# Seven early norms: the factor as a power on GpSimd in place of a root on ScalarE and a reciprocal on VectorE

## The chip, the cores and the metric

The kernel runs on one core of one Trainium2 chip. The metric is the device time of one execution in microseconds (us), the median of several runs. Less is better. The engines are TensorE (PE in the rows; PEld is its weight load), VectorE (DVE), ScalarE (ACT), GpSimd (POOL) and SyncE (SP), which issues most of the loads.

## The reference, cut to what matters

The reference is two transformer-like blocks on 512 tokens with a model width of 1024, all in float32. Every sublayer begins with a root-mean-square norm over the width:

```python
def rms_norm(x, g):
    xf = x.astype(jnp.float32)
    y = xf * lax.rsqrt(jnp.mean(xf * xf, axis=-1, keepdims=True) + EPS)
    return (y * g.astype(jnp.float32)).astype(x.dtype)
```

The norms that the change touches stand before the two feed-forward parts of the first block, before its short convolution, at its end (`norm_one`), and in the second block before the cross attention, before the feed-forward part and at the end. What follows a norm is, but for `norm_one` and the last one, a product of all 1024 normalised columns with a weight matrix, so no product can begin before the norm has its factor.

## The kernel before, in words

Activations are kept transposed: the 128 partitions hold columns of the model, the free dimension holds the 512 tokens, and the 1024 columns are KD = 8 tiles of 128 x 512. `X` is the residual stream. `XN` is the normalised tile, and it lies in the buffer `HXF`, as do the squares of a norm before it. `XNH` and `XNL` are its high and low parts: the products are made of three float32r products, high by high, low by high and high by low (`split_product`, L688 to L690, and for the first two units after a norm `split_pair`, L703 to L705). The weights are split on VectorE into `WH` (L714) and `WL` (L716), one unit of 128 x 1024 at a time, two units ahead of TensorE. SyncE loads the weights into a ring of slots.

Each engine has its own program, and the order of work on each engine is the order in which it is written there; engines meet only at semaphores. A `NormStage` holds the semaphores and the steps of one norm. In a norm with `early=True` the work goes so:

- ScalarE writes the square of each tile of `X` as it is finished (L596, `norm_act_squares`), eight squares.
- GpSimd adds squares 1 to 6 onto square 0 (L625, `norm_pool`), six additions, each after the one before and after its square.
- TensorE multiplies the sum and square 7 by a matrix of ones (L634, `norm_pe`), so that each partition of bank 6 holds the sum over the whole width for the 512 tokens.
- ScalarE takes the root of that sum over 1024 plus EPS into `ROOT` (L600, `norm_act_root`).
- VectorE takes the reciprocal of `ROOT` into `RSTD` (L640, `norm_dve`) and then multiplies the eight tiles of `X` by `RSTD` (L649, where a gain and a shift are applied by ScalarE at L608, and L651, where the gain is applied in the same instruction). The low parts (L647) are put between these multiplications; ScalarE makes the high parts (L617).

`RSTD` and `ROOT` are one buffer each of 768 columns, and all norms share them. Eleven norms go through `norm_act_root` and `norm_dve`. The seven with `early=True` are `norm_ffn[0]`, `norm_sc`, `norm_ffn[1]`, `norm_one`, `norm_x2`, `norm_ffn2` and `norm_last`; the four others (`norm_lat`, `norm_ctx`, `norm_mix2`, `norm_mem2`) have no part on GpSimd. Of the latter, `norm_mix2` follows `norm_one` directly, and `norm_mem2` follows `norm_x2` on VectorE and ScalarE.

GpSimd's program has little else in these stretches. The four norms of the first block stand one after another in one loop, after them come the masks of the recurrent layer (L941) and four loads by DMA, and then the three norms of the second block. A sequence of additions in that program waits for ScalarE's squares, as it does before.

The lines from 1205 to 1265 and from 1515 to 1615 are TensorE's program around the norms, in the order `feed_forward(0)`, `norm_sc`, the short convolution, `feed_forward(1)`, `norm_one`, `norm_mix2`, then the recurrent and the attention layer, and then `norm_x2`, the cross attention, `norm_ffn2`, the feed-forward part, `norm_last` and the transposes of the output (L1617).

Of the kernel before, what the change touches and what calls it, by code (L numbers as in the profile page):

```python
# [8 lines left out]
ALU = mybir.AluOpType  # L9
ACT = mybir.ActivationFunctionType  # L10
# [4 lines left out]
P = 128  # L15
D = 1024
KD = D // P
T = 512
# [93 lines left out]
class Progress:  # L112
# [4 lines left out]
    def __init__(self, sem, steps, loop=False):  # L117
        self.sem, self.steps, self.n = sem, steps.split(), len(steps.split())
        self.credit, self.at = self.n if loop else 0, 0
# [88 lines left out]
class NormStage:  # L208
# [3 lines left out]
    def __init__(self, prog, name, shifted, parts=False, early=False):  # L212
        ks = range(KD)
        act = [[f"mod{k}"] if shifted else [] for k in ks]
        dve = [[f"n{k}"] for k in ks]
        for k in ks if parts else ():
            act[min(k + 1, KD - 1)].append(f"hi{k}")
            dve[min(k + 3, KD - 1)].append(f"l{k}")
        self.act_steps, self.dve_steps = sum(act, []), sum(dve, [])
        self.act = prog(f"{name}_act", " ".join([f"sq{k}" for k in ks] + ["root"] + self.act_steps))  # L220
        self.pe = prog(f"{name}_pe", "ssq")
        self.dve = prog(f"{name}_dve", " ".join(["rstd"] + self.dve_steps))
        self.pool = prog(f"{name}_pool", " ".join(f"a{k}" for k in range(1, KD - 1))) if early else None
        self.shifted = shifted

        self.out = self.act if shifted else self.dve
        self.written = self.out.done(f"mod{KD - 1}" if shifted else f"n{KD - 1}")
# [21 lines left out]
def two_blocks(nc, a, consts_d, bias_d, out):  # L249

    ctx = ExitStack()
    with ctx:
        def sb(name, n, parts=P):
            return ctx.enter_context(nc.sbuf_tensor(name, [parts, n], F32))

        def sem(name):
            return ctx.enter_context(nc.semaphore(name))

        def prog(name, steps, loop=False):
            return Progress(sem(name), steps, loop)  # L260
# [25 lines left out]
        bank = [PS[:, b, :] for b in range(8)]  # L286

        def banks(b, n):

            return PS[:, b:b + n, :].rearrange("p b n -> p (b n)")  # L290
# [11 lines left out]
        HX = HXF[:, :].rearrange("p (k t) -> p k t", k=KD)  # L302
        XN = cut(HXF, 0, KD, T)
        W = sb("W", SLOTS * SLOT)[:, :].rearrange("p (s n) -> p s n", s=SLOTS)
        EPSC = sb("EPSC", 3)
        ROOT, RSTD = sb("ROOT", TA), sb("RSTD", TA)
        SILU_C = sb("SILU_C", 2 * KD)[:, :].rearrange("p (k w) -> p k w", w=2)
        MOD = sb("MOD", 2 * N_MOD)
# [271 lines left out]
        def start_credit(eng, which):  # L580
            for p in LOOPS[which]:
                eng.sem_inc(p.sem, p.credit)


        def norm_act(act, st, src, sq, tokens, b, dst=None, gain=None, shift=None, ready=None):


            norm_act_squares(act, st, src, sq, ready)
            norm_act_root(act, st, tokens, b)
            norm_act_out(act, st, dst, gain, shift)  # L590
# [6 lines left out]

        def norm_act_root(act, st, tokens, b):
            act.wait_ge(st.pe.sem, st.pe.done("ssq"))
            nc.scalar.activation(ROOT[:, 0:tokens], bank[b][:, 0:tokens], ACT.Sqrt,  # L600
                                             bias=EPSC[:, 0:1], scale=1.0 / D).then_inc(st.act.sem, st.act.step("root"))

        def norm_act_out(act, st, dst=None, gain=None, shift=None):
# [15 lines left out]
        def norm_pool(pool, st, sq):  # L619

            for k in range(1, KD - 1):
                pool.wait_ge(st.act.sem, st.act.done(f"sq{k}"))
                if k > 1:
                    pool.wait_ge(st.pool.sem, st.pool.done(f"a{k - 1}"))
                nc.gpsimd.tensor_tensor(sq[:, 0, :], sq[:, 0, :], sq[:, k, :], ALU.add).then_inc(st.pool.sem, st.pool.step(f"a{k}"))  # L625

        def norm_pe(pe, st, sq, tokens, b):

            for k in (0, KD - 1) if st.pool else range(KD):
                if st.pool and k == 0:  # L630
                    pe.wait_ge(st.pool.sem, st.pool.done(f"a{KD - 2}"))
                else:
                    pe.wait_ge(st.act.sem, st.act.done(f"sq{k}"))
                mm = nc.tensor.matmul(bank[b][:, 0:tokens], ONES, sq[:, k, :], start=(k == 0), stop=(k == KD - 1))  # L634
            mm.then_inc(st.pe.sem, st.pe.step("ssq"))

        def norm_dve(dve, st, src, dst, tokens, gain=None):

            dve.wait_ge(st.act.sem, st.act.done("root"))
            nc.vector.reciprocal(RSTD[:, 0:tokens], ROOT[:, 0:tokens]).then_inc(st.dve.sem, st.dve.step("rstd"))  # L640
            dve.wait_ge(st.dve.sem, st.dve.done("rstd"))
            for step in st.dve_steps:
                k = int(step[1:])
                if step.startswith("l"):
                    dve.wait_ge(st.act.sem, st.act.done(f"hi{k}"))
                    normed, hi, lo = st.split
                    ins = nc.vector.tensor_tensor(lo[:, k, :], normed[:, k, :], hi[:, k, :], ALU.subtract)  # L647
                elif st.shifted:
                    ins = nc.vector.tensor_tensor(dst[:, k, :], src[:, k, :], RSTD[:, 0:tokens], ALU.mult)  # L649
                else:  # L650
                    ins = nc.vector.scalar_tensor_tensor(dst[:, k, :], src[:, k, :], gain[:, k:k + 1], RSTD[:, 0:tokens],  # L651
                                                         ALU.mult, ALU.mult)
                ins.then_inc(st.dve.sem, st.dve.step(step))
# [220 lines left out]
        def _(pool):  # L874
# [53 lines left out]
                        DT["dta"][:, d, 0:NT, ds(i * 2 + e, 1)].broadcast_to([P, NT, P]), ALU.mult).then_inc(sl_pool.sem, sl_pool.step(f"d{q}"))  # L928
            for st in (norm_ffn[0], norm_sc, norm_ffn[1], norm_one):
                norm_pool(pool, st, XN)  # L930


            def level_masks(i, at, p_pe, p_dve, p_pool):
# [21 lines left out]
                    nc.gpsimd.dma_start(DBIAS[:, e, :, :], by_pair[i, e]).then_inc(dbias_in, 16)  # L955
            for st in (norm_x2, norm_ffn2, norm_last):
                norm_pool(pool, st, XN)

        @block.tensor
        def _(pe):  # L960
# [26 lines left out]


            norm_pe(pe, norm_lat, XN_SQ, T, 6)
            norm_pe(pe, norm_ctx, CX_SQ, TC, 5)  # L990

            pe.wait_ge(in_act.sem, in_act.done("cols"))
# [629 lines left out]
        def _(act):  # L1622
# [21 lines left out]
            norm_act_squares(act, norm_lat, X, XN_SQ)  # L1644
            norm_act_squares(act, norm_ctx, CX, CX_SQ)
            norm_act_root(act, norm_lat, T, 6)
            act.wait_ge(norm_lat.dve.sem, norm_lat.dve.done("rstd"))
            norm_act_root(act, norm_ctx, TC, 5)
            act.wait_ge(ada_dve.sem, ada_dve.done("gainc"))
            norm_act_out(act, norm_lat, HX[:, :, 0:T], GAIN[:, 0, :], MOD[:, 0:KD])  # L1650
# [5 lines left out]
            for j in range(NPAIR):  # L1656
# [5 lines left out]

                nc.scalar.activation(ROOT[:, 0:T], bank[6], ACT.Sqrt, bias=EPSC[:, 1:2]).then_inc(hy_act.sem, hy_act.step(f"root{j}"))
            act.wait_ge(freed[ring.slot("hy_in", 8)], ring.used("hy_in", 8))
            nc.scalar.activation(KRAW, banks(4, 2)[:, 0:TA], ACT.Copy).then_inc(hy_act.sem, hy_act.step("k"))
            nc.scalar.activation(KSQ, banks(4, 2)[:, 0:TA], ACT.Square).then_inc(hy_act.sem, hy_act.step("ksq"))
            act.wait_ge(hy_pe.sem, hy_pe.done("kssq"))
            nc.scalar.activation(ROOT[:, 0:TA], banks(6, 2)[:, 0:TA], ACT.Sqrt, bias=EPSC[:, 0:1], scale=1.0 / HEAD).then_inc(hy_act.sem, hy_act.step("kroot"))

# [59 lines left out]
            for g in range(2):  # L1729
                act.wait_ge(gn_pe.sem, gn_pe.done(f"ssq{g}"))  # L1730
                nc.scalar.activation(DIFF[:, g, :], bank[g], ACT.Sqrt, bias=EPSC[:, 0:1], scale=1.0 / (2 * P)).then_inc(gn_act.sem, gn_act.step(f"root{g}"))

# [72 lines left out]
            def pair_pass(i, at, p_pe, p_act, p_dve, ahead):  # L1805
# [36 lines left out]
                act.wait_ge(p_pe.sem, p_pe.done("var", at))  # L1842
                nc.scalar.activation(ROOT[:, 0:T], bank[1], ACT.Sqrt, bias=EPSC[:, 2:3], scale=1.0 / HEAD).then_inc(p_act.sem, p_act.step("groot"))

# [95 lines left out]
        def _(dve):  # L1940
            start_credit(dve, "dve")
            nc.vector.memset(EPSC[:, 0:1], EPS)
            nc.vector.memset(EPSC[:, 1:2], HEAD * EPS).then_inc(in_dve.sem, in_dve.step("eps"))
            def ada_step(name, u, i, k, sums, before):

                s = ring.slot(name, u)
                dve.wait_ge(landed[s], ring.arrived(name, u, i))
                if u >= before:
                    dve.wait_ge(freed[ring.slot(name, u - before)], ring.used(name, u - before, i))
                else:  # L1950
                    dve.wait_ge(freed[ring.slot(name, u - before)], ring.free(name, u - before + SLOTS, i))
                nc.vector.scalar_tensor_tensor(sums, W[:, s, 0:D], SILU_C[:, ds(k, 1), 0], sums, ALU.mult, ALU.add).then_inc(freed[s], 1)
# [4 lines left out]
            for block, name in enumerate(("ada_shift", "ada_scale")):  # L1957
                with dve.Fori(0, 2) as i:
                    for u in range(4):
                        s, k, at = ring.slot(name, u), i * 4 + u, i + 2 * block  # L1960
# [54 lines left out]
            for j in range(XBC_TILES):  # L2015
                dve.wait_ge(freed[ring.slot("hy_in", 9 + j)], ring.used("hy_in", 9 + j))
                b = 2 * (j % 3)
# [242 lines left out]
            with dve.Fori(0, 2) as i:  # L2260
                for f in range(4):
                    b, o = 3 * (f % 2), CV[:, f % 2, :]
# [52 lines left out]
            r, k, v = (PRKV[:, u, :] for u in range(3))  # L2315
# [164 lines left out]
            with dve.Fori(0, KD) as i:  # L2480
                for u in range(4):
# [3 lines left out]
                    name, gate = (("r", SGR), ("a", SGA))[u - 2]  # L2485
# [86 lines left out]
```

## Time and profile before

| | |
|---|---|
| Time, median of three runs | 3348.53 us (3348.12 to 3349.93) |
| The profiled execution's own time | 3347.87 us |
| Its span, first to last instruction | 3346.2 us |
| Mean granted TensorE clock | 0.911 of full speed |
| PE, DVE, ACT and POOL busy | 89%, 49%, 20% and 6% of the span |
| Reciprocals of the norms (L640) | 11, nine of them over 512 tokens |
| Additions of squares on GpSimd (L625) | 42, mean 1.285 us |

The profile's page shows busy time and the chain of work that ended last. The chain is followed back from the last instruction to whatever released each step, so a piece that stands in it was not covered by anything else. In the timeline a row gives the start, the length, the engine, the line and the operation, and in brackets how long the engine had been idle and what ended that. The execution's own time is 1.67 us above its span.

### The profile page before, as it was taken

The numbers are of one execution on the slowest core, as the hardware profiler recorded it, in microseconds if no ns is written. First come the engines' busy times: TensorE is split into PE (matmuls) and PEld (weight loads), VectorE is DVE, ScalarE is ACT, GpSimd is POOL, SyncE is SP. The second block draws the span as 40 slices with busy tenths as digits, with TensorE's granted clock in tenths as the row PEclk, the third lists the DMA queues.
The fourth block names the chain that finished last, engine by engine and source line by source line (L and its number), as shares of the span: only waits on it lengthen the run. The fifth ranks groups of instructions, "written<-read, shape, count | busy, mean of one in ns | idle before, by whom it ended". The sixth has DMA issues, their size and how long they took to land.

```text
span 3346.2 us, 44820 instructions
## 1 busy us (share of the span) xinstructions
PE 2977.0 (89%) x17401; PEld 2135.4 (64%) x17401; DVE 1642.6 (49%) x2188; ACT 671.3 (20%) x1114; POOL 189.8 (6%) x227
## 2 busy tenths in 40 slices
PE   5998886799998989999879898888969988889998
PEld 3453464388886878888445555545537766768886
DVE  7555556344445554444356555622045453355554
ACT  3212321121101021110223333312131121121111
POOL 3010011000000000000001100100000000000000
PEclk8987666899999999999989999987969989999999
DMA  7443400233332323333110011020203322223332
GB/s 241 144 143 115 131 24 0 63 88 90 95 95 84 94 76 94 94 95 93 41 29 22 23 36 29 22 70 25 67 12 82 91 69 70 69 81 95 94 94 69
DMA packets 406147, 255.20 MB, mean 76 GB/s; under 512 B 23863, under 2 KB 391056, under 8 KB 405904
## 3 DMA queue, kind: packets, MB, share of 16 engines
q1 hardware_dynamic: 397824, 226.85, 23.4%
q0 software_dynamic: 6928, 21.89, 2.0%
q10 hardware_dynamic: 1280, 4.78, 0.4%
q8 instruction: 90, 1.47, 0.2%
q14 instruction: 25, 0.20, 0.0%
HBM read 250.60 MB, written 2.10 MB: 76 GB/s over the span
## 4 chain that ended last, share of the span: by engine, by line
PE 83%; DVE 9%; issue 4%; ACT 2%; DMA 1%; DVEq 0%; POOL 0%; ACTq 0%; POOLq 0%; SPq 0%
PE PS L688 12%; PE PS L690 12%; PE PS L689 12%; PE PS L675 9%; PE PS L1297 5%; PE PS L703 3%; PE PS L705 3%; PE PS L704 3%; PE PS L1083 2%; PE PS L1474 1%; PE PS L1466 1%; PE PS L1372 1%; PE PS L1064 1%; PE PS L1340 1%; PE PS L1074 1%
## 5 line engine op out<-in xcount | busy, mean ns | idle before, releaser
L714 DVE CAST WH<-W 128x1024 fp32r<-128x1024 f32 x304 | 210.9, 694 | 724.0 <-PE PS L690 551.1
L716 DVE TENSOR_TENSOR WL<-W,WH 128x1024 fp32r<-128x1024 f32 x304 | 372.7, 1226 | 10.4
L689 PE MATMUL PS<-XNL,WH 128*128 128x512 f32 x864 | 340.6, 394 | 0.0
L675 PE MATMUL PS<-HXF,W 128*128 128x512 f32 (+2 forms) x640 | 260.2, 567 | 19.9 <-ACT HXF L608 7.1
L690 PE MATMUL PS<-XNH,WL 128*128 128x512 f32 x704 | 277.5, 394 | 0.0
L688 PE MATMUL PS<-XNH,WH 128*128 128x512 f32 x704 | 277.3, 394 | 0.0
L689 PE MATMUL PS<-HL,WH 128*128 128x512 f32 x672 | 261.5, 389 | 0.0
L688 PE MATMUL PS<-HH,WH 128*128 128x512 f32 x672 | 261.5, 389 | 0.0
L690 PE MATMUL PS<-HH,WL 128*128 128x512 f32 x672 | 261.4, 389 | 0.0
L675 PEld LDWEIGHTS PS<-HXF,W 128*128 128x128 f32 (+1 forms) x640 | 122.6, 193 | 157.3 <-issue 152.1
L703 PE MATMUL PS<-XNH,WH 128*128 128x512 f32 x448 | 180.6, 403 | 32.8 <-DVE XNL L647 32.8
L704 PE MATMUL PS<-XNL,WH 128*128 128x512 f32 x480 | 193.5, 403 | 0.0
L689 PEld LDWEIGHTS PS<-XNL,WH 128*128 128x128 f32 x864 | 162.5, 188 | 38.3
L1297 PE MATMUL PS<-HXF,W 128*128 128x512 f32 x336 | 172.7, 653 | 11.5 <-DVE ARENA L2358 11.5
L705 PE MATMUL PS<-XNH,WL 128*128 128x512 f32 x448 | 179.1, 400 | 0.0
L625 POOL TENSOR_TENSOR HXF<-HXF 128x512 f32<-128x512 f32 x42 | 54.0, 1285 | 1965.3 <-ACT HXF L596 1965.3
L690 PEld LDWEIGHTS PS<-XNH,WL 128*128 128x128 f32 x704 | 132.2, 188 | 31.2
L688 PEld LDWEIGHTS PS<-XNH,WH 128*128 128x128 f32 x704 | 132.2, 188 | 31.0
L688 PEld LDWEIGHTS PS<-HH,WH 128*128 128x128 f32 x672 | 126.1, 188 | 26.3
L689 PEld LDWEIGHTS PS<-HL,WH 128*128 128x128 f32 x672 | 126.1, 188 | 26.3
L690 PEld LDWEIGHTS PS<-HH,WL 128*128 128x128 f32 x672 | 126.1, 188 | 26.2
L596 ACT ACTIVATE HXF<-X 128x512 f32<-128x512 f32 x72 | 44.7, 630 | 459.2 <-DVE X L2243 227.3
(454 smaller groups left out, 4818.5 us busy)
## 6 DMA issues: line engine op xcount, KB each, us to landing
W<-in_ada_w SPq DMA_DIRECT2D x64, 512.0 KB, 4.2
W<-in_ffn_w SPq DMA_DIRECT2D x64, 512.0 KB, 4.1
W<-in_w_in SPq DMA_DIRECT2D x58, 512.0 KB, 3.9
W<-in_ffn_w_gate SPq DMA_DIRECT2D x44, 512.0 KB, 3.8
W<-in_ffn_w_up SPq DMA_DIRECT2D x44, 512.0 KB, 3.8
ARENA<-in_ada_w POOLq DMA_DIRECT2D x32, 512.0 KB, 5.0
W<-in_ffn_w_down SPq DMA_DIRECT2D x32, 512.0 KB, 4.0
W<-in_sc_w_in SPq DMA_DIRECT2D x24, 512.0 KB, 3.7
```

Of the source, the lines that this page charges most:

```text
L625: nc.gpsimd.tensor_tensor(sq[:, 0, :], sq[:, 0, :], sq[:, k, :], ALU.add).then_inc(st.pool.sem, st.pool.step(f"a{k}"))
L675: mm = nc.tensor.matmul(dst, w[:, k, :], rhs(k), start=(start and k == 0), stop=(stop and k == kts - 1))
L688: nc.tensor.matmul(dst, WH[:, h, c], hi(k), start=(start and k == 0), stop=False)
L689: nc.tensor.matmul(dst, WH[:, h, c], lo(k), start=False, stop=False)
L690: mm = nc.tensor.matmul(dst, WL[:, h, c], hi(k), start=False, stop=(stop and k == kts - 1))
L703: nc.tensor.matmul(dst[u], WH[:, h, c], hi(k), start=(k == 0), stop=False)
L704: nc.tensor.matmul(dst[u], WH[:, h, c], lo(k), start=False, stop=False)
L705: mm = nc.tensor.matmul(dst[u], WL[:, h, c], hi(k), start=False, stop=(k == KD - 1))
L714: nc.vector.tensor_copy(WH[:, h, :], W[:, s, 0:D]).then_inc(parted, 1)
L716: nc.vector.tensor_tensor(WL[:, h, :], W[:, s, 0:D], WH[:, h, :], ALU.subtract).then_inc(freed[s], 1)
L1083: mm = nc.tensor.matmul(bank[6][h, :], VT[:, c, h], PT[:, e, c, :], start=(c == 0), stop=(c == NA - 1))
L1297: mm = nc.tensor.matmul(bank[7], tiles(s)[:, k, :], xn(k), start=(k == 0), stop=(k == KD - 1))
```

## The change

The seven norms with `early=True` have a step `rstd` on GpSimd in place of VectorE's. The change's description counts eight norms; the two loops that call the new function name seven. ScalarE's instruction at L600 stays, with the function Identity in place of Sqrt, so that `ROOT` then holds mean plus EPS. GpSimd raises that to the power of -0.5, which it reads from a fourth column of `EPSC`, broadcast over the tokens. VectorE waits for that in place of taking a reciprocal. The four other norms keep the root and the reciprocal.

```diff
-        self.dve = prog(f"{name}_dve", " ".join(["rstd"] + self.dve_steps))
-        self.pool = prog(f"{name}_pool", " ".join(f"a{k}" for k in range(1, KD - 1))) if early else None
+        self.dve = prog(f"{name}_dve", " ".join(([] if early else ["rstd"]) + self.dve_steps))
+        self.pool = prog(f"{name}_pool", " ".join([f"a{k}" for k in range(1, KD - 1)] + ["rstd"])) if early else None
...
-        EPSC = sb("EPSC", 3)
+        EPSC = sb("EPSC", 4)
...
-            nc.scalar.activation(ROOT[:, 0:tokens], bank[b][:, 0:tokens], ACT.Sqrt,
+            nc.scalar.activation(ROOT[:, 0:tokens], bank[b][:, 0:tokens], ACT.Identity if st.pool else ACT.Sqrt,
                                              bias=EPSC[:, 0:1], scale=1.0 / D).then_inc(st.act.sem, st.act.step("root"))
...
+        def norm_power(pool, st, tokens):
+
+            pool.wait_ge(st.act.sem, st.act.done("root"))
+            nc.gpsimd.tensor_tensor(RSTD[:, 0:tokens], ROOT[:, 0:tokens], EPSC[:, 3:4].broadcast_to([P, tokens]), ALU.pow).then_inc(st.pool.sem, st.pool.step("rstd"))
+
...
-            dve.wait_ge(st.act.sem, st.act.done("root"))
-            nc.vector.reciprocal(RSTD[:, 0:tokens], ROOT[:, 0:tokens]).then_inc(st.dve.sem, st.dve.step("rstd"))
-            dve.wait_ge(st.dve.sem, st.dve.done("rstd"))
+            if st.pool:
+                dve.wait_ge(st.pool.sem, st.pool.done("rstd"))
+            else:
+                dve.wait_ge(st.act.sem, st.act.done("root"))
+                nc.vector.reciprocal(RSTD[:, 0:tokens], ROOT[:, 0:tokens]).then_inc(st.dve.sem, st.dve.step("rstd"))
+                dve.wait_ge(st.dve.sem, st.dve.done("rstd"))
...
             for st in (norm_ffn[0], norm_sc, norm_ffn[1], norm_one):
                 norm_pool(pool, st, XN)
+                norm_power(pool, st, T)
...
             for st in (norm_x2, norm_ffn2, norm_last):
                 norm_pool(pool, st, XN)
+                norm_power(pool, st, T)
...
+            nc.vector.memset(EPSC[:, 3:4], -0.5)
```

## Rows read from the trace of the kernel before

**Rows 1.** The page: busy time, and the chain by engine.

```profile
PE 2977.0 (89%) x17401; PEld 2135.4 (64%) x17401; DVE 1642.6 (49%) x2188; ACT 671.3 (20%) x1114; POOL 189.8 (6%) x227
PE 83%; DVE 9%; issue 4%; ACT 2%; DMA 1%; DVEq 0%; POOL 0%; ACTq 0%; POOLq 0%; SPq 0%
```

**Rows 2.** The chain of waits, whole span: start us, us, what.

```profile
659.72 3.27 DVE RSTD L640
...
1038.98 3.36 DVE RSTD L640
1230.75 3.37 DVE RSTD L640
1609.01 3.37 DVE RSTD L640
...
2721.35 3.37 DVE RSTD L640
...
2963.95 3.36 DVE RSTD L640
...
3328.98 3.37 DVE RSTD L640
```

**Rows 3.** Timeline around norm_sc: start us, us, engine, line, operation.

```profile
1036.96 1.28 ACT L600 ACT_TABLE_LOAD   x1
...
1037.00 1.12 PE L634 MATMUL PS<-HXF,CONST 128*128 128x512 f32 x2 [2.51 <-ACT HXF L596]
1038.26 0.69 ACT L600 ACTIVATE ROOT<-PS,EPSC 128x512 f32<-128x512 f32 x1
1038.98 3.35 DVE L640 RECIPROCAL RSTD<-ROOT 128x512 f32<-128x512 f32 x1 [2.69 <-ACT ROOT L600]
1042.37 2.50 DVE L649 TENSOR_TENSOR HXF<-X,RSTD 128x512 f32<-128x512 f32 x4
...
1046.00 0.77 PE L703 MATMUL PS<-XNH,WH 128*128 128x512 f32 x1 [7.88 <-DVE XNL L647]
```

**Rows 4.** Timeline around the first norm, norm_ffn[0].

```profile
657.87 0.69 ACT L600 ACTIVATE ROOT<-PS,EPSC 128x512 f32<-128x512 f32 x1 [1.22 <-PE PS L634]
...
659.63 3.35 DVE L640 RECIPROCAL RSTD<-ROOT 128x512 f32<-128x512 f32 x1
...
663.02 2.50 DVE L649 TENSOR_TENSOR HXF<-X,RSTD 128x512 f32<-128x512 f32 x4
```

**Rows 5.** Instructions of L640 and L600: count, ns min/median/max, first and last start.

```profile
L640 DVE RECIPROCAL RSTD<-ROOT x11: 1744/3352/3354, 52.2 to 3329.0; 128x512 f32<-128x512 f32 x9, 128x256 f32<-128x256 f32 x2
L600 ACT ACT_TABLE_LOAD  x5: 1283/1283/1283, 34.9 to 2961.9; - x5
```

**Rows 6.** Groups on POOL: busy us, mean ns, idle before, releaser.

```profile
L625 POOL TENSOR_TENSOR HXF<-HXF 128x512 f32<-128x512 f32 x42 | 54.0, 1285 | 1965.3 <-ACT HXF L596 1965.3
L926 POOL TENSOR_TENSOR ARENA<-CONST,ARENA 128x512 f32<-128x512 f32 x16 | 21.8, 1379 | 54.9 <-PE PS L1146 54.8
...
L903 POOL MEMSET HXF<- 128x6144 f32 x1 | 5.2, 5218 | 0.4 <-PE PS L1049 0.4
```

**Rows 7.** Timeline: a square on ACT and the addition on POOL behind it.

```profile
2706.96 0.63 ACT L596 ACTIVATE HXF<-X 128x512 f32<-128x512 f32 x1 [4.81 <-DVE X L2501]
...
2707.67 1.29 POOL L625 TENSOR_TENSOR HXF<-HXF 128x512 f32<-128x512 f32 x1 [4.15 <-ACT HXF L596]
```

**Rows 8.** Timeline: a POOL instruction and the DVE instruction that followed its end.

```profile
223.84 5.22 POOL L903 MEMSET HXF<- 128x6144 f32 x1 [0.38 <-PE PS L1049]
...
229.27 0.96 DVE L2041 TENSOR_REDUCE ARENA<-PS 128x1 f32<-128x768 f32 x1 [4.08 <-POOL HXF L903]
```

**Rows 9.** Stretches around norm_ffn[1]: busy us, instructions, PEclk, DMA share, GB/s.

```profile
1231.00:1237.00 6.00, 0.00 (x0) 0.00 (x0) 5.66 (x6) 2.14 (x4) 0.00 (x0) 0.50 0.00 0
1238.00:1244.00 6.00, 6.00 (x15) 4.53 (x16) 5.22 (x9) 6.00 (x11) 0.00 (x0) 0.51 0.00 0
1244.00:1252.00 8.00, 8.00 (x36) 6.47 (x35) 3.23 (x5) 2.66 (x4) 0.00 (x0) 1.00 0.01 4
```

## The prediction

> **What bounds the kernel now.** I read the page first. TensorE is busy for 89% of the span and makes 83% of the chain that ended last, with VectorE at 9% and GpSimd at 0% [rows 1]. So the kernel is bound by TensorE over most of its length, and a change of VectorE's or GpSimd's work can only count where TensorE stands still. The second view is the chain of waits over the whole span, to see whether the places of the change are such. They are: seven pieces of it are the reciprocal of L640 in the seven early norms, 3.27 us in the first and 3.36 or 3.37 us in the six others [rows 2]. Nothing covers them. The third view is the timeline of one norm [rows 3]. After the ones product ends at 1038.12 (1037.00 plus 1.12) the order is strictly serial: root, reciprocal, first normalised tile, and TensorE is idle for 7.88 us until 1046.00. The reader is to see that the reciprocal is 3.35 us of this gap, and that everything which takes its place will be in the gap too, at its full length.
>
> **What the change removes.** In six of the seven norms the time from the end of the root to the start of the first normalised tile is 1042.37 - (1038.26 + 0.69) = 3.42 us, which is the reciprocal and two handovers of 0.03 us [rows 3]; rows 2 show the same length in all six. In the first norm the reciprocal starts late, because VectorE still splits weights: the root ends at 657.87 + 0.69 = 658.56, the reciprocal starts at 659.63 and the first tile at 663.02, which is 4.46 us [rows 4]. GpSimd has no such queue there, so the 1.07 us of lateness goes too. The sum is 6 x 3.42 + 4.46 = 25.0 us.
>
> The root becomes an Identity of the same shape on the same engine. I give it the same 0.69 us; a difference of more than 0.1 us either way would be 0.7 us in all. Its table load goes in four of the seven norms (five loads at L600, the first at 34.9 us being that of the very first norm [rows 5]). But the load lies beside the ones product: it ends at 1038.24, the product at 1038.12 and the root starts at 1038.26 [rows 3], so at most 0.14 us a piece is won, 0.6 us in all. The load then has to come ahead of the roots that stay, where ScalarE mostly waits anyway. Between 0 and 0.6 I take 0.2 us.
>
> At this place the Trainium skill prices higher. "ScalarE: Activation LUTs", section "What ACT_TABLE_LOAD costs", gives 1283 ns for a load and about 1380 ns for a drain beside it; four switches at about 2.66 us would make 10.6 us of gain. The trace agrees on the 1283 ns [rows 5] but shows the root starting 0.02 us after the load's end [rows 3], so no such drain is in the gap, and the measurement decides.
>
> **What it adds.** One power of 128x512 on GpSimd in each of the seven norms, and one handover more. From ScalarE to GpSimd the handover is 2707.67 - (2706.96 + 0.63) = 0.08 us [rows 7]. From GpSimd to VectorE the nearest row has 229.27 - (223.84 + 5.22) = 0.21 us [rows 8], for an instruction that only followed; the handovers between other engines take 0.03 us [rows 3]. I take 0.10 us, together 0.18 us a norm, 1.3 us in all (0.8 to 2.0).
>
> The time of the power, T, is the whole question, and no row shows a power. From below: GpSimd's addition of two 128x512 operands takes 1.285 us [rows 6], and its multiplication of the same shape with an operand read by broadcast 1.379 us [rows 6]. A power can't be cheaper than the cheapest thing done to the same two operands, so T is at least 1.29 us. From above there is no true bound in the trace, so I count arithmetic. A power of general exponent has to split off the exponent of the base, take a logarithm of the rest, multiply, split the product again, take an exponential and see to the special cases. In float32 accuracy each of the two functions is a polynomial of six to eight terms, so it is about 26 operations on every element, my count. What is one such operation worth on GpSimd? Its memset writes 6144 columns in 5.218 us, which is 0.435 us for 512 columns [rows 6]; that is the price of one pass in which every column is touched once. With the first operation at the addition's full price and 25 more at 0.435 us, T is 1.285 + 25 x 0.435 = 12.2 us. If each of the 26 cost what a whole addition costs, reads and write included, T would be 26 x 1.285 = 33.4 us. VectorE's reciprocal is a hint in the same direction: 3.35 us against 0.63 us for a multiplication of that shape (four in 2.50 us) [rows 3] says that one function of one operand is already worth five simple operations on the other engine; five times 1.285 us would be 6.4 us, and a power is at least two functions, 12.9 us. I take 12.2 us and keep 1.29 and 33.4 as the ends.
>
> **The sum.** Change = 7 T + 1.3 - 25.0 - 0.2 = 7 T - 23.9 us. With T = 12.2 it is +61.5 us. The profiled execution took 3347.87 us (its span of 3346.2 and 1.67 around it), so the same execution would take 3409.4 us. It lies 0.66 us below the median of the runs, which makes the forecast 3410 us, 1.8% slower.
>
> **What lies around it.** While VectorE waits for the power, its eight tile multiplications and the split of the next weights are queued behind, as they are now behind the reciprocal; they move by the same amount, and TensorE waits for the low part behind them. On GpSimd nothing is queued that anyone needs: its next work is the next norm's additions or, after `norm_one`, the masks of the recurrent layer, which wait for VectorE. SyncE's loads of weights only get more time. TensorE's clock: in the gap it is granted half speed (0.50 from 1231 to 1237, the level of 1.2 GHz), it stays there for the first 6 us of the products (0.51 from 1238 to 1244), and is full, 2.4 GHz, after that [rows 9]. A gap longer by 9 us begins and ends in the same state, and the low clock is already paid for. Whether it lasts a little more or less behind a longer gap I can't read; a bound is 2 us either way for each of the six norms that products follow, 12 us, and I take 0.
>
> **Rivals.**
>
> A. The power costs about what an addition costs, T = 1.3 to 2.4, and the kernel is faster. At T = 1.29 the change is 9.0 - 23.9 = -14.9 us, 3333.6 us. For it: GpSimd's addition is short [rows 6], and the place is the best there is, on the chain seven times [rows 2]. Against it: the two operands of an addition are most of its cost, and this rival gives the 25 other operations for nothing. The point from which it decides is T = 23.9 / 7 = 3.4 us, where the kernel breaks even: the reciprocal's own length.
>
> B. The operations of the power issue several at once, so that it ends near the reciprocal. At three per pass, 26 operations cost 26 x 0.435 / 3 = 3.8 us, the change is +2.7 us, and the time 3351 us. For it: the memset's 0.435 us is one write per column, and nothing in the rows says that only one operation fits into it. Against it: the operations of a polynomial wait for one another. The Trainium skill has this rule: "GPSIMD Engine Reference", section "3.1 Elementwise — side-by-side cycle accounting", says that a loop body of three and more operations is bound by instruction slots at roughly 3 operations per cycle. No row of this trace shows it.
>
> C. Each operation costs as much as an addition, or the function is done with branches: T from 25 us, at 33.4 us the change is +209.9 us, 3558 us. For it: the addition and the multiplication both cost three times the memset's price per column [rows 6]. Against it: those pay for operands that a power reads once.
>
> That the change does not do what it says is small: if the compiler kept a table load at L600, 0.2 us would be missing.
>
> **How the numbers follow.** I give the forecast's case, T from 4.4 to 25 us with 12.2 as its value, 0.57; its own range is 3355 to 3499 us. A has 0.13, B (T from 2.5 to 4.4) 0.09, C 0.21. A measurement of this kernel can tell about 0.2%, 6.7 us, from no change: faster by more than that needs T below 2.5, slower needs T above 4.4. So faster has 0.13, the same 0.09, slower 0.78. The range takes in the lower end with A and its handovers and the upper end at T = 33.4: 3332 to 3560 us; only what lies above T = 33.4, some 0.13 to 0.15, and little else is left out.
>
> **What would show it.** In the profile of the changed kernel L640 has four instructions in place of eleven. A new line on POOL has seven, reading `ROOT` and writing `RSTD`; their duration is T, and it should be 12 us. The chain of waits should have seven pieces of it where L640 stood, and VectorE's idle time ahead of L649 and L651 should name it as releaser. ScalarE's L600 should have no load but for the norms that stay, and the rows of the products should be unchanged. If the span grows by 7 T - 24 with the T that is read there, the mechanism is right whatever T is; if T is off, only that term is. The prediction is wrong if T is below 4.4 us, or if the gaps grow by less than the power's length, which would mean that the power overlaps something.

## The result and the profile after

The changed kernel takes 3899.3 us (median, 3897.2 to 3900.0) against 3348.6 us before: a ratio of 1.1643, 95% interval 1.1623 to 1.1663. It is 550.7 us slower. The forecast of 3410 us had the sign right and the size wrong by nine times (+61.5 us), and the time lies far above its range of 3332 to 3560 us.

The page of the changed kernel, busy time and the chain by engine and by line, against [rows 1]:

```profile
PE 2976.0 (76%) x17401; PEld 2134.4 (55%) x17401; DVE 1619.1 (42%) x2182; ACT 654.6 (17%) x1101; POOL 764.2 (20%) x234
...
PE 71%; POOL 13%; DVE 7%; issue 4%; POOLq 2%; ACT 2%; DMA 1%; DVEq 0%; ACTq 0%; SPq 0%
```

TensorE's work is the same to 1 us, so its share falls only because the span grows. GpSimd's busy time rises by 574.4 us, and GpSimd, which was at 0% of the chain, is 15% of it with its queue. The seven instructions behind this are those of the new line L630 (first row), and the reciprocal has four left, as against eleven in [rows 5] (second row):

```profile
L630 POOL TENSOR_TENSOR RSTD<-ROOT,EPSC x7: 81927/81928/82903, 658.5 to 3799.7; 128x512 f32<-128x512 f32 x7
...
L648 DVE RECIPROCAL RSTD<-ROOT x4: 1752/2550/3353, 52.3 to 3127.5; 128x512 f32<-128x512 f32 x2, 128x256 f32<-128x256 f32 x2
```

One power takes 81.93 us, 0.160 us for each column of 128 elements, and six of the seven agree to 0.01 us; the first takes 82.90 us. In the chain of waits (start us, us, what) they stand where the reciprocals of [rows 2] stood; the last of the seven is put down to GpSimd's queue:

```profile
658.48 82.91 POOL RSTD L630
1117.32 81.94 POOL RSTD L630
1387.68 81.94 POOL RSTD L630
...
1844.39 81.94 POOL RSTD L630
...
3035.27 81.95 POOL RSTD L630
...
3356.00 81.94 POOL RSTD L630
...
3799.62 81.97 POOLq L252
```

The timeline of `norm_sc` in the changed kernel, against [rows 3]:

```profile
1115.39 1.12 PE L639 MATMUL PS<-HXF,CONST 128*128 128x512 f32 x2 [2.51 <-ACT HXF L596]
1116.55 0.69 ACT L600 ACTIVATE ROOT<-PS,EPSC 128x512 f32<-128x512 f32 x1 [1.22 <-PE PS L639]
1117.32 81.93 POOL L630 TENSOR_TENSOR RSTD<-ROOT,EPSC 128x512 f32<-128x512 f32 x1 [15.58 <-ACT ROOT L600]
...
1199.28 2.50 DVE L657 TENSOR_TENSOR HXF<-X,RSTD 128x512 f32<-128x512 f32 x4 [84.61 <-POOL RSTD L630]
...
1202.92 0.76 PE L711 MATMUL PS<-XNH,WH 128*128 128x512 f32 x1 [86.40 <-DVE XNL L655]
```

The reader is to see three things. The table load is gone, and the Identity follows the product by 0.04 us where the root followed it by 0.14. The handovers are 1117.32 - (1116.55 + 0.69) = 0.08 us to GpSimd and 1199.28 - (1117.32 + 81.93) = 0.03 us from it. And TensorE's gap has grown from 7.88 to 86.40 us, that is 78.52 us, by as much, to 0.1 us, as the way from ScalarE to VectorE has: from 3.42 to 1199.28 - 1117.24 = 82.04 us.

### The profile page after: what moved, and what is told of

Same layout as the page of the kernel before. It is cut to its first block, busy times and chain, and to the rows that moved or that the text cites. A ratio compares the mean times of both kernels' runs of the same rounds, so it can differ in the third digit from the quotient of the medians.

```text
span 3895.4 us, 44808 instructions
## 1 busy us (share of the span) xinstructions
PE 2976.0 (76%) x17401; PEld 2134.4 (55%) x17401; DVE 1619.1 (42%) x2182; ACT 654.6 (17%) x1101; POOL 764.2 (20%) x234
## 4 chain that ended last, share of the span: by engine, by line
PE 71%; POOL 13%; DVE 7%; issue 4%; POOLq 2%; ACT 2%; DMA 1%; DVEq 0%; ACTq 0%; SPq 0%
POOL RSTD L630 13%; PE PS L696 10%; PE PS L698 10%; PE PS L697 10%; PE PS L683 8%; PE PS L1307 4%; PE PS L711 3%; PE PS L713 3%; PE PS L712 3%; POOLq L252 2%; PE PS L1093 2%; PE PS L1484 1%; PE PS L1476 1%; PE PS L1382 1%; PE PS L1074 1%
## 5 line engine op out<-in xcount | busy, mean ns | idle before, releaser
L630 POOL TENSOR_TENSOR RSTD<-ROOT,EPSC 128x512 f32<-128x512 f32 x7 | 574.5, 82069 | 61.9 <-ACT ROOT L600 61.9
L724 DVE TENSOR_TENSOR WL<-W,WH 128x1024 fp32r<-128x1024 f32 x304 | 372.7, 1226 | 10.4
L711 PEld LDWEIGHTS PS<-XNH,WH 128*128 128x128 f32 x448 | 85.7, 191 | 372.9 <-issue 349.6
L950 POOL TENSOR_TENSOR ARENA<-ARENA,CONST 128x256 f32<-128x256 f32 x80 | 54.1, 691 | 524.5 <-DVE ARENA L2383 399.2
L696 PEld LDWEIGHTS PS<-XNH,WH 128*128 128x128 f32 x704 | 132.2, 188 | 31.0
```

What stands on the lines that cost most here:

```text
L630: nc.gpsimd.tensor_tensor(RSTD[:, 0:tokens], ROOT[:, 0:tokens], EPSC[:, 3:4].broadcast_to([P, tokens]), ALU.pow).then_inc(st.pool.sem, st. ...
L696: nc.tensor.matmul(dst, WH[:, h, c], hi(k), start=(start and k == 0), stop=False)
L711: nc.tensor.matmul(dst[u], WH[:, h, c], hi(k), start=(k == 0), stop=False)
L724: nc.vector.tensor_tensor(WL[:, h, :], W[:, s, 0:D], WH[:, h, :], ALU.subtract).then_inc(freed[s], 1)
```

## The experiments

The diffs below are shortened: lines can begin inside a call, and semaphore steps and declarations are left out.

**1. The place without the power.**

```diff
-ROOT[:, 0:tokens], EPSC[:, 3:4].broadcast_to([P, tokens]), ALU.pow)
+ROOT[:, 0:tokens], EPSC[:, 3:4].broadcast_to([P, tokens]), ALU.add)
...
-bias=EPSC[:, 0:1], scale=1.0 / D)
+bias=EPSC[:, 0:1], scale=(1e-6 if st.pool else 1.0) / D)
...
-nc.vector.memset(EPSC[:, 3:4], -0.5)
+nc.vector.memset(EPSC[:, 3:4], 0.1)
```

> GpSimd adds 0.1 to every element in place of raising it to a power, and ScalarE scales the mean by a millionth so that the factor stays near 0.1: the factor itself is left out, every place and wait of the change is kept. Theory 1 (the length of the power is all that was mis-sized): the instruction takes 1.3 to 1.4 us, and the sum 7 T - 23.9 gives -14.5 us against the kernel before, 3334 us. Theory 2 (the place costs something too: a second wait, the queue of GpSimd, the clock): the kernel is not faster by more than 5 us although T is small.

Measured: 3333.8 us against 3349.7 us for the kernel before beside it, ratio 0.9955 (0.9939 to 0.9972). The row of the addition at the power's place:

```profile
L630 POOL TENSOR_TENSOR RSTD<-ROOT,EPSC 128x512 f32<-128x512 f32 x7 | 8.2, 1171 | 62.6 <-ACT ROOT L600 62.6
```

With T = 1.17 us the sum 7 T - 23.9 gives -15.7 us; measured are -15.9 us in the time (interval -20.4 to -9.4) and 3330.2 - 3346.2 = -16.0 us in the span. Theory 1 holds: with a short instruction in the same place the kernel is faster, and the large miss is in T. The addition itself took 1.04 us in six norms and 1.97 us in the first, less than the 1.3 to 1.4 us expected; so the 1.285 us that the prediction took as T's lower end is no lower end for an operand read by broadcast.

That the sum is met to 0.3 us is in part luck. In the traces, from the root of the first norm to the end, this kernel is 17.6 us shorter than the one before. From one changed norm's root to the next it is shorter by 1.0, 2.3, 3.0, 7.5, 0.0, 1.8 and 2.1 us in order, where the sum has 2.4 for the first and 2.3 for each other; what makes up the 7.5 was not separated. The time from root to first tile did fall as priced, by 2.28 us in `norm_sc` (4.11 to 1.83). What moved too is the granted clock: the ones product of `norm_sc`, which is not changed, takes 1.86 us in place of 1.12 [rows 3], with the clock at 0.50 from 1038 to 1039 us.

```profile
1036.99 1.86 PE L639 MATMUL PS<-HXF,CONST 128*128 128x512 f32 x2 [2.51 <-ACT HXF L596]
```

**2. What the length of a power hangs on.** Each norm has another shape, in the order of the program:

```diff
+RSTD[:, 0:256], ROOT[:, 0:256], minus_half(P, 256)
+RSTD[:, 0:4], ROOT[:, 0:4], minus_half(P, 4)
+RSTD[0:1, 0:512], ROOT[0:1, 0:512], minus_half(1, 512)
+RSTD[:, 0:512], ROOT[:, 0:512], EPSC[:, 4:5].broadcast_to([P, 512])
+RSTD[:, 0:512], ROOT[:, 0:512], HALF
+RSTD[0:16, 0:512], ROOT[0:16, 0:512], minus_half(16, 512)
+RSTD[:, 0:128], ROOT[:, 0:128], minus_half(P, 128)
```

`EPSC[:, 4:5]` holds 1.0 and `HALF` is a full tile of -0.5.

> Each of the seven norms has the power in another shape; the rest of the factor is left as it stood in the buffer, so this is computed only in part. In order: 256 columns, 4 columns, 1 partition of 512 columns, 512 columns with exponent 1.0, 512 columns with the exponent from a full tile of -0.5 in place of a broadcast, 16 partitions of 512 columns, 128 columns. Theory P (a fixed number of instructions for each column, all lanes of a core at once): 0.160 us a column whatever the partitions, so 41, 0.6 to 1, 82, 82, 82, 82 and 20.5 us, sum 389 us, total about 3348.5 + 389 + 1.3 - 25 = 3714 us. Theory L (lane after lane within each of the cores): the single partition takes a sixteenth, 5 us, and 16 partitions 82 us. Theory V (the price hangs on the values): the exponent 1.0 is shorter by more than a fifth. Theory B (the broadcast operand makes it slow): the full tile is far shorter than 82 us. Theory S (a start cost in each call, such as loading code): 4 columns take over 10 us and 256 columns more than half of 82.

Measured: 3718.8 us, one run, against about 3714 expected. The seven instructions in order (count, ns min/median/max, start):

```profile
L635 POOL TENSOR_TENSOR RSTD<-ROOT,EPSC x1: 42102/42102/42102, 660.6 to 660.6; 128x256 f32<-128x256 f32 x1
L637 POOL TENSOR_TENSOR RSTD<-ROOT,EPSC x1: 1023/1023/1023, 1078.6 to 1078.6; 128x4 f32<-128x4 f32 x1
L639 POOL TENSOR_TENSOR RSTD<-ROOT,EPSC x1: 81926/81926/81926, 1269.5 to 1269.5; 1x512 f32<-1x512 f32 x1
L641 POOL TENSOR_TENSOR RSTD<-ROOT,EPSC x1: 81937/81937/81937, 1725.5 to 1725.5; 128x512 f32<-128x512 f32 x1
L643 POOL TENSOR_TENSOR RSTD<-ROOT,HALF x1: 82159/82159/82159, 2914.4 to 2914.4; 128x512 f32<-128x512 f32 x1
L645 POOL TENSOR_TENSOR RSTD<-ROOT,EPSC x1: 81926/81926/81926, 3238.9 to 3238.9; 16x512 f32<-16x512 f32 x1
L647 POOL TENSOR_TENSOR RSTD<-ROOT,EPSC x1: 20727/20727/20727, 3682.5 to 3682.5; 128x128 f32<-128x128 f32 x1
```

One partition takes what 128 take, so the time doesn't grow with the partitions (L falls). The exponent 1.0 takes what -0.5 takes (V falls), the full tile even 0.2 us more than the broadcast (B falls), and 4 columns 1.02 us (S falls). From 128 and 512 columns the slope is (81.93 - 20.73) / 384 = 0.1594 us a column and the rest 0.33 us. The 256 columns fit that but for 1.0 us, for which see experiment 6. So of the five theories P is left, as far as its price goes: T is a price by the column, 0.1594 us where the memset's is 5.218 / 6144 = 0.00085 us, 188 times as much. That it is a fixed number of instructions is not shown; no run counts them.

**3. The same power, on ScalarE.** From the kernel before:

```diff
-nc.scalar.activation(ROOT[:, 0:tokens], bank[b][:, 0:tokens], ACT.Sqrt,
+nc.scalar.activation(ROOT[:, 0:tokens], bank[b][:, 0:tokens], ACT.Ln if st.pool else ACT.Sqrt,
                                  bias=EPSC[:, 0:1], scale=1.0 / D)
+if st.pool:
+    act.wait_ge(st.act.sem, st.act.done("root"))
+    nc.scalar.activation(RSTD[:, 0:tokens], ROOT[:, 0:tokens], ACT.Exp, scale=-0.5)
```

> From the kernel before: in the same seven norms ScalarE forms the factor by itself, as the exponential of -0.5 times the logarithm of mean plus eps, two instructions of 0.69 us, in place of root, handover and reciprocal. If the gap costs its full length on the chain, as the sum assumed, each norm saves 4.11 - (0.69 + 0.03 + 0.69) = 2.7 us where both functions are in one set of tables, and 1.4 us where a table load of 1.28 us stands between them; the first norm saves 1.1 us more. Sum -20 us (3328 us) or -11 us (3337 us). The rival that the gaps are covered by something else behind them: within 3 us of 3348.5.

Measured: 3340.0 us against 3349.7 us, ratio 0.9972 (0.9961 to 0.9983). The chain of waits in `norm_sc`:

```profile
1038.03 1.82 PE PS L637 x2
1039.88 0.69 ACT ROOT L600
1040.58 1.28 ACT L604
1041.87 0.64 ACT RSTD L604
1042.54 0.70 DVE HXF L655
```

A table load of 1.28 us stands between the logarithm and the exponential, so it is the expected case with the load. From the logarithm's end to the first tile it is 1042.54 - 1040.57 = 1.97 us against 3.42, which is 1.45 us in each of six norms; in the first the way from root to tile fell from 5.15 to 2.66 us, 2.49 less. Together that is 11.2 us, measured are 9.7 (interval 5.7 to 13.1). This version beats both kernels, by a small amount.

**4 and 5. Only the distinct values.** The sum that the ones product makes is the same on all 128 partitions, so 512 columns hold only 512 distinct numbers. Two kernels carry the sum to where it stands only once for each token, in six norms:

```diff
-mm = nc.tensor.matmul(bank[b][:, 0:tokens], ONES, sq[:, k, :], start=(k == 0), stop=(k == KD - 1))
+for t in range(NT):
+    mm = nc.tensor.matmul(bank[b][:, 2 * t:2 * t + 2], sq[:, k, t * P:(t + 1) * P], ONES[:, 0:2], ...)
...
+nc.vector.tensor_tensor(DG, mid(IDENT, NT), last(RSTD[:, 0:2 * NT:2], P), ALU.mult)
...
+nc.tensor.matmul(bank[st.spread_bank], ONES, DG.rearrange("p n t -> p (n t)"), start=True, stop=True)
```

`DG` is the unit matrix times the factor of each token. Between the sum and `DG` experiment 4 has GpSimd's power on 8 columns, experiment 5 the root and the reciprocal on 8 columns.

> From the kernel before, in six of the seven norms (the last one stays): TensorE takes the squares as weights, so that the sum of a token stands once, tokens over the partitions, in 8 columns (4 sums, each twice), in place of 512 columns repeated on all partitions. GpSimd raises those 8 columns to the power -0.5, VectorE multiplies the unit matrix by them, and TensorE spreads them over the partitions again with the matrix of ones. The law of the second experiment, 0.33 + 0.1594 us a column, gives 1.6 us for the power in place of 81.9. The rest of the path: products 1.0, Identity 0.25, handovers 0.2, unit matrix 0.7, spreading 1.0. Path 4.8 us against 5.37 us before, so about -0.6 x 6 = -3 us: 3345 us. If the power has a high price of its own however few the columns, it is slower than before.

Measured: 3358.9 us against 3349.0 us, ratio 1.0030 (1.0019 to 1.0041). Its power:

```profile
L637 POOL TENSOR_TENSOR RSTD<-ROOT,EPSC x6: 1646/1650/1850, 658.5 to 2971.4; 128x8 f32<-128x8 f32 x6
```

The law of experiment 2 gave 1.6 us, measured 1.65: it holds down to 8 columns, and the other 540 us of the change are gone. But the expectation of -3 us missed by 13 us. In `norm_sc` the path from the last product's start to the first tile takes 6.79 us, not 4.8: the products take 1.86 us in place of 1.0 and the spreading 2.07 in place of 1.0. Over the six norms this path sums to 39.3 us against 33.9 before, which is 5.4 of the measured 9.9 us; where the other 4.5 us arise was not separated. Experiment 5 was expected so:

> As the kernel with the power on 8 columns, but the 8 columns go through ScalarE's root (0.25 us) and VectorE's reciprocal (0.12 us). Path: products 1.0, root 0.25, reciprocal 0.15, unit matrix 0.7, spreading 1.0, handovers 0.2, in all 3.3 us against 5.37, so -2.1 us a norm, -12 to -13 us in six norms: 3337 us. Rival: TensorE has the low clock in the gap and the products and the spreading cost twice that, with fp32 weights that are loaded for two columns each; then the path is 4.5 to 5 us and the gain under 5 us.

Measured: 3345.2 us against 3349.0 us, ratio 0.9990 (0.9981 to 0.9999), a tenth of a percent, at the very edge of what can be told. The rival holds in its gain under 5 us and in the low clock. Its timeline in `norm_sc`:

```profile
1038.86 1.87 PE L643 MATMUL PS<-CONST,HXF 128*128 128x2 f32 x8 [2.58 <-ACT HXF L599]
1040.76 0.27 ACT L604 ACTIVATE ROOT<-PS,EPSC 128x8 f32<-128x8 f32 x1 [0.66 <-PE PS L643]
1041.06 0.20 DVE L655 RECIPROCAL RSTD<-ROOT 128x8 f32<-128x8 f32 x1 [2.92 <-ACT ROOT L604]
1041.30 0.69 DVE L659 TENSOR_TENSOR DG<-CONST,RSTD 128x512 f32<-128x512 f32 x1
...
1042.05 2.07 PE L649 MATMUL PS<-DG,CONST 128*128 128x512 f32 x2 [1.32 <-DVE DG L659]
1044.16 2.48 DVE L669 TENSOR_TENSOR HXF<-X,PS 128x512 f32<-128x512 f32 x4 [2.16 <-PE PS L649]
```

The two parts of TensorE take 1.87 and 2.07 us in place of the 1.0 each that was expected, both with the clock granted at 0.50. Eight products of the same form that ran 3.5 us earlier, at 1.00, took 0.95 us:

```profile
1035.33 0.95 PE L643 MATMUL PS<-CONST,HXF 128*128 128x2 f32 x8
```

The path from the start of these last products to the first tile is 5.30 us against 5.37 (1042.37 - 1037.00) before. The reciprocal fell from 3.35 to 0.20 us and the root from 0.69 to 0.27, 3.57 us in all; the unit matrix (0.69), the spreading (2.07) and the longer products (1.87 against 1.12) took 3.51 us back. The six norms differ: the path is 4.48 to 6.01 us here, 5.27 to 6.31 before, and 2.7 us shorter over all six.

**6. The power beside the work, not waited for.** From the kernel before, in six norms:

```diff
+pool.wait_ge(st.act.sem, st.act.done("root"))
+nc.gpsimd.tensor_tensor(SPARE, EPSC[:, 4:5].broadcast_to([P, T]), EPSC[:, 3:4].broadcast_to([P, T]), ALU.pow)
```

> From the kernel before, root and reciprocal as they are. In six of the seven norms (not the last) GpSimd also raises 512 columns to the power -0.5 after the root, into a buffer that nobody reads: 6 x 82 = 492 us of GpSimd's time beside the work. Theory 1 (the wait on the chain is the whole price): within 2 us of the kernel before, 3346 to 3352 us. Theory 2 (GpSimd at work slows VectorE or TensorE, by a shared port or by the clock): VectorE's split of the weights, 1.226 us each before, is longer where the power runs, and the kernel is more than 7 us slower.

Measured: 3349.7 us against 3348.9 us, ratio 1.0001 (0.9991 to 1.0011). The power on GpSimd, and VectorE's split of the weights over the whole span:

```profile
L631 POOL TENSOR_TENSOR SPARE<-EPSC 128x512 f32<-128x512 f32 x6 | 492.9, 82147 | 56.1 <-ACT ROOT L601 56.1
L722 DVE TENSOR_TENSOR WL<-W,WH 128x1024 fp32r<-128x1024 f32 x304 | 372.7, 1226 | 10.4
```

`EPSC[:, 4:5]` holds 2.0 here, so this power of one constant takes as long as that of the norms' means. 492.9 us of GpSimd's time cost nothing measurable, and the split keeps its 1226 ns. Theory 1 holds: it is the wait that costs. The traces say it more sharply than the times: from the first norm's root to the end it is 2688.3 us in both kernels.

The first norm's power is 82.90 us here as in the changed kernel. It begins while VectorE is in the middle of a split. In experiment 1, where the instruction is short, that is plain:

```profile
660.06 1.23 DVE L724 TENSOR_TENSOR WL<-W,WH 128x1024 fp32r<-128x1024 f32 x1
660.21 1.97 POOL L630 TENSOR_TENSOR RSTD<-ROOT,EPSC 128x512 f32<-128x512 f32 x1 [7.51 <-ACT ROOT L600]
...
1229.15 1.04 POOL L630 TENSOR_TENSOR RSTD<-ROOT,EPSC 128x512 f32<-128x512 f32 x1 [6.06 <-ACT ROOT L600]
```

The addition takes 1.97 us where 1.08 us of it overlap with the split (660.21 to 661.29), and 1.04 us where VectorE stands still. No run moves the split away, and how the one delays the other is not shown: it is not the overlap by itself, since in experiment 6 four of the later powers run beside 12 or 13 splits each and take 81.93, 81.93, 81.94 and 82.25 us, and in experiment 4 the first power of 8 columns, with a whole split beside it, takes 1.85 us in place of 1.65. That the first power in a program would cost 1 us more by itself is ruled out by the next experiment.

**7. The change in three norms.**

```diff
+power = self.power = early and name in ("norm_x2", "norm_ffn2", "norm_last")
-bias=EPSC[:, 0:1] ... ACT.Identity if st.pool else ACT.Sqrt
+bias=EPSC[:, 0:1] ... ACT.Identity if st.power else ACT.Sqrt
```

> The change undone in the four norms of the first block and kept in the three of the second. If every norm pays the length of its power less 3.42 us, independent of the others: 3 x (81.95 + 0.09 - 3.42) = +236 us, and about 1 us more for the first call in the program: 3585 to 3587 us. If part of the price was due to the norms following one another, or the first block's norms cost more, it is off by more than 5 us.

Measured: 3585.4 us against 3348.9 us, +236.5 us, ratio 1.0707 (1.0686 to 1.0728). The norms pay independently, 78.8 us each, and the four that are left out are worth the other 314 us of the 550.7. Its first power, which begins with VectorE idle, takes 81.97 us, so the 1 us for a first call was wrong:

```profile
2723.37 81.97 POOL L631 TENSOR_TENSOR RSTD<-ROOT,EPSC 128x512 f32<-128x512 f32 x1 [6.99 <-ACT ROOT L601]
```

## Why the prediction was wrong

**The step that failed.** It is "T is 1.285 + 25 x 0.435 = 12.2 us". T is 81.93 us. The count of 26 operations was mine and had no row, and neither had the step of giving each operation the memset's price; what the instruction costs is 188 memset prices a column. Which of the two was off, the number of operations or the price of one, no run can tell apart. The step behind it failed too: the upper end of 33.4 us took 26 as given and only raised the price of one operation, so it was no bound at all, and the 0.13 to 0.15 of chance above it rested on no row. The price by the column was the same whatever partitions, exponent (-0.5 or 1.0) or operand form (experiment 2), and for a constant base (experiment 6); nothing tried brought 512 columns near 12 us. Why a column costs 0.159 us inside the instruction is open; the trace doesn't show it.

**Rivals.** A (below 3.4 us) and B (3.8 us) both fall. B took three operations a pass and the same count of 26. The rule it named, in the Trainium skill's "GPSIMD Engine Reference", section "3.1 Elementwise — side-by-side cycle accounting", is of roughly 3 operations per cycle for longer loop bodies; no run here shows it or speaks against it, and without the number of operations it gives no time. C had the right direction, was put from 25 us up and named branches or dear operations; its value of 33.4 us was two and a half times too small.

**What was right.** The sum 7 T - 23.9 us with the measured 7 T = 574.5 us gives +550.6 us; measured are +550.7 us in the time (interval +543 to +557) and +549.2 us in the span. The first agreement is closer than the times can tell. Its parts, one by one:

- All seven places are on the chain, at full length: seven pieces again. From one changed norm's root to the next, and from the last to the end, the changed kernel's trace is longer by 78.1 to 78.6 us each time; the length of the power plus 0.11 us of handovers less 3.42 us (4.46 in the first) is 78.6 us.
- 25.0 us go: the ways from root to first tile show it, and experiment 1 agrees in its total, though not stretch by stretch.
- The handovers are 0.08 and 0.03 us, not 0.08 and 0.10, which is 0.5 us in all.
- The table load was worth 0.1 us in `norm_sc`, inside the bound of 0.14 a piece. Four such loads make 0.4 us, where 0.2 was taken. With this and the handovers the sum is +549.9 us.
- Nothing on GpSimd's queue was needed: experiment 6 has it busy for 493 us more at no cost.
- The low clock is already paid for, as taken. Around `norm_ffn[1]` of the changed kernel, where TensorE's gap is 86.4 us long as well, the stretches read as in [rows 9] (busy us of the five engines with counts, then PEclk, DMA share and GB/s):

```profile
1390.00:1465.00 75.00, 0.00 (x0) 0.00 (x0) 0.00 (x0) 0.00 (x0) 75.00 (x1) 0.50 0.00 0
1473.00:1479.20 6.20, 5.92 (x14) 4.58 (x15) 5.67 (x10) 6.20 (x12) 0.00 (x0) 0.50 0.00 0
1479.20:1487.00 7.80, 7.80 (x35) 6.29 (x35) 3.27 (x5) 1.68 (x4) 0.00 (x0) 1.00 0.00 0
```

The products begin at 1473.3 and have the full clock from 1479.2 on, 6 us, as after the gap of 7.8 us. The 6 us that the prediction gave to all six norms are those of this one alone: in order of the five norms that products follow directly, the low clock lasts 3.9, 3.5, 6.1, 3.9 and 3.5 us before and 3.9, 3.4, 6.1, 3.9 and 3.9 us after. A gap eleven times as long costs hardly anything more at its end.

## What to carry to other kernels

Split a forecast into a part that the trace prices and the one price that it doesn't: here the sum was right within what the runs can tell once T was read, and T alone was off by nearly seven times. For an instruction that no row shows, an own count of its arithmetic gives no upper end; leave the top open, or say from which T on the answer changes (3.4 us here) and put one such instruction on the chip first. Look for the same value repeated over partitions or columns, but price the way there and back: in `norm_sc` the 3.57 us saved on root and reciprocal were eaten by 0.69 us for a unit matrix, 2.07 for the spreading and 0.75 more for the products, while two table functions on the engine that already held the number gained 9.7 us. And where a change is worth 2 us a place, check it at every place: a total that fits can be made of stretches that don't.

## What the runs showed that I had not expected

- GpSimd's power costs 0.33 us and 0.1594 us a column, the same for 1, 16 and 128 partitions, for the exponents -0.5 and 1.0, and for a broadcast or a full second operand. At 4 columns it is 1.02 us, at 8 it is 1.65 us, at 512 it is 81.93 us.
- GpSimd's addition of a tile and a broadcast column takes 1.04 us with VectorE idle and 1.97 us when it begins beside VectorE's split of two operands. A power of 82 us takes 1.0 us more for the same start; later splits beside it, in experiment 6, cost nothing in three norms and 0.3 us in one.
- ScalarE took a table load of 1.28 us between a logarithm and an exponential that follow each other directly.
- Eight products of TensorE took 0.95 us with the clock granted at 1.00 and 1.87 us at 0.50. In short gaps the point where the clock falls is not fixed: the unchanged ones product of `norm_sc` took 1.12 us before and 1.86 us in experiment 1, after the same idle time of 2.51 us.
